# Reordering the mixing stage and the layer boundary of a two-block transformer

## The chip, the core and the metric

One core of a Trainium2 chip runs the whole program. The metric is the device time of one execution in microseconds. The kernel before was timed three times: 1442.81, 1445.81 and 1448.04, median 1445.81.

## What is computed

Two blocks of two layers each work on the same x of 256 rows (SEQ) by 1024 (D_MODEL), in float32. The change lies in the first block and at the start of the second. Of a layer of the first block, this matters:

```python
h = rms_norm(x, norm_mix[l])
proj = h @ w_in[l]                     # q, k, v of two attentions, and gate_logits
y_a = dilated_attention(dq, dk, dv) @ w_proj_a[l]               # 256 wide output, then 1024
y_b = stick_breaking_attention(sq, sk, sv) @ w_proj_b[l]
gates = jax.nn.sigmoid(gate_logits + b_gate[l])
mixed = gates[..., :D_MODEL] * y_a + gates[..., D_MODEL:] * y_b
x = x + mixed @ w_out[l]
h = rms_norm(x, norm_ffn[l])
x = x + conv_ffn(h, w_up[l], conv_w[l], conv_b[l], w_down[l])
```

After the two layers x is normalized, and the second block begins. It also normalizes a memory (256 rows) and multiplies it with weights into keys and values for a later cross attention.

## The kernel before

**Numbers in two parts.** Every float32 operand of a large product is split into a high part (rounded to fp32r) and a low part, the rest. A product is three matmuls: high by high, high by low weight, low by high weight. Activations are 256 rows, two tiles (tt) of 128; their parts are in ahi and alo, or in mhi and mlo, eight blocks of 128 columns each.

**Weights.** They come in chunks of 1 MB through three buffers (raw), in the order of a plan made ahead; SP asks for chunk n once both halves of chunk n-3 are split. Each chunk has two halves of 1024 columns per partition. ACT makes a half's high part (split_half, L1603) and DVE the low one (L2044), each into one of four slots (HL); ACT waits until PE is done with the half four before. Both engines call split_half(m) at written places in their programs, which splits every half up to m that is not split yet. Counted from f0, the first half of the gates' weights, halves 16 and 17 belong to projection b, 18 and 19 to projection a, 20 to 23 to the first column half of w_out ("out1", 0) and 24 to 27 to its second.

**Turning.** PE needs activations turned. A stream turns four groups of four 128 by 128 blocks (turn_blocks, L1005, into PSUM bank 4 or 5), ACT copies a group's high part out (stream_hi), DVE its low part (stream_lo), and PE waits for the low part of the group that the next half chunk needs. turn_to(i) turns all groups up to i; half_chunk calls need before and turn_to after its products, two groups ahead.

**Order.** The program of each engine is written out by hand, and an instruction stands behind all those written before it. Semaphores tie the engines together. Around the change, in one layer of the first block:

1. PE runs the dilated attention. Between its units it does gate products and the product with w_proj_b (between_heads, two half chunks of 12 matmuls). DVE then normalizes the attention output into o_nat (L2161).
2. PE turns branch a (four blocks), ACT takes the high part (L1635), DVE the low (L2081). PE waits for it, then runs w_proj_a as column_chunk (L970 to L972): columns 0 to 511 and then 512 to 1023, in each the two weight halves outside and the two row tiles inside, so that both tiles of a column end together.
3. ACT applies one sigmoid to the gates of branch b (L1759), takes the turned branch a, splits two weight halves, and applies the other sigmoid (L1762). DVE multiplies gates and products: branch b in place (L2299), branch a into o_nat (L2306), and adds the two (L2310, which raises "mixed").
4. PE turns the mixed blocks (stream "mix", into mhi and mlo) and runs out1: groups 0 and 1 ahead of the first half chunk, groups 2 and 3 behind the first and second. DVE's order is: split 20, mix column 0, split 21, low parts of groups 0 and 1, mix column 1, splits 22 and 23, low parts of groups 2 and 3.
5. DVE adds the product to x (L2330). PE turns x for the feed-forward part (stream "xf"), runs it, and ends with the last "down" chunk, also a column_chunk. DVE adds it to x (L2420), PE turns x for the next layer (stream "x1"), and DVE's low parts (L2071) let the next layer's first product (L897) begin.

At the start of the second block, ACT scales the memory's values (memory_product, L1700) in layer 0 ahead of the high parts of the stream "x2" (L1628, L1629).

## Time and profile before

| what | value |
|---|---|
| median of 3 runs | 1445.81 us |
| profiled execution, own time | 1443.27 us |
| its span, first to last instruction | 1441.4 us |
| PE, PEld busy | 1398.6 us, 1190.4 us |
| DVE, ACT, POOL busy | 1016.5 us, 737.9 us, 91.0 us |
| mean granted TensorE clock | 0.998 |
| read from HBM | 239.09 MB |

The profile shows one execution. PE's busy time counts pipelined matmuls whose ends are modelled: one of 512 columns lasts 0.39 us in the records while the next starts 0.23 after it. So the starts are what counts, and the idle time in brackets behind a row is the gap after the modelled end. An arrow in those brackets names the engine and the line that ended the gap.

### The profile page before, as it was taken

The numbers are of one execution on the slowest core, as the hardware profiler recorded it, in microseconds if no ns is written. First come the engines' busy times: TensorE is split into PE (matmuls) and PEld (weight loads), VectorE is DVE, ScalarE is ACT, GpSimd is POOL, SyncE is SP. The second block draws the span as 40 slices with busy tenths as digits, with TensorE's granted clock in tenths as the row PEclk, the third lists the DMA queues.
The fourth block names the chain that finished last, engine by engine and source line by source line (L and its number), as shares of the span: only waits on it lengthen the run. The fifth ranks groups of instructions, "written<-read, shape, count | busy, mean of one in ns | idle before, by whom it ended". The sixth has DMA issues, their size and how long they took to land.

```text
span 1441.4 us, 20319 instructions
## 1 busy us (share of the span) xinstructions
PE 1398.6 (97%) x7936; PEld 1190.4 (83%) x7936; DVE 1016.5 (71%) x1525; ACT 737.9 (51%) x1126; POOL 91.0 (6%) x94
## 2 busy tenths in 40 slices
PE   8999999999999999999999999899999999899997
PEld 6899888888788988888887777788888877788886
DVE  5566678777755657877787676786676657786665
ACT  4563555555455454554555565554445455554443
POOL 0000001000000000211012011100000000100000
PEclk9999999999999999999999999999999999999999
DMA  9734446565454425756647304368865505265552
GB/s 298 248 121 147 135 159 203 179 203 201 153 199 153 140 88 176 240 190 198 204 176 212 111 30 146 104 204 221 220 188 188 175 1 173 91 205 176 194 193 81
DMA packets 154434, 242.36 MB, mean 168 GB/s; under 512 B 4506, under 2 KB 107050, under 8 KB 154076
## 3 DMA queue, kind: packets, MB, share of 16 engines
q1 hardware_dynamic: 150624, 227.23, 48.2%
q0 software_dynamic: 3712, 13.84, 3.7%
q8 instruction: 63, 1.03, 0.3%
q14 instruction: 31, 0.25, 0.1%
q10 hardware_dynamic: 4, 0.01, 0.0%
HBM read 239.09 MB, written 1.97 MB: 167 GB/s over the span
## 4 chain that ended last, share of the span: by engine, by line
PE 90%; DVE 5%; ACT 2%; POOL 1%; issue 1%; DMA 0%; SPq 0%; DVEq 0%; ACTq 0%; POOLq 0%
PE ps L931 19%; PE ps L897 16%; PE ps L904 16%; PE ps L901 16%; PE ps L934 9%; PE ps L1005 3%; PE ps L1083 2%; PE ps L1059 2%; PE ps L1074 1%; DVE wlo L2044 1%; PE ps L970 1%; PE ps L972 1%; PE ps L971 1%; POOL rstd L759 1%; ACT whi L1603 1%
## 5 line engine op out<-in xcount | busy, mean ns | idle before, releaser
L2044 DVE TENSOR_TENSOR wlo<-raw,whi 128x1024 fp32r<-128x1024 f32 (+1 forms) x432 | 539.2, 1259 | 208.1 <-ACT whi L1603 207.6
L1603 ACT CAST whi<-raw 128x1024 fp32r<-128x1024 f32 (+1 forms) x432 | 446.0, 1042 | 269.8 <-PE ps L904 167.8
L931 PE MATMUL ps<-act,whi 128*128 128x512 f32 x1184 | 324.9, 395 | 1.7 <-DVE wlo L2044 1.3
L897 PE MATMUL ps<-whi,mhi 128*128 128x512 f32 (+2 forms) x688 | 236.4, 392 | 4.0 <-DVE mlo L2068 2.2
L931 PEld LDWEIGHTS ps<-act,whi 128*128 128x128 f32 x1184 | 204.8, 189 | 32.4 <-DVE wlo L2044 2.0
L904 PE MATMUL ps<-whi,mlo 128*128 128x512 f32 (+2 forms) x688 | 231.3, 385 | 0.0
L901 PE MATMUL ps<-wlo,mhi 128*128 128x512 f32 (+2 forms) x688 | 231.1, 385 | 0.0
L934 PEld LDWEIGHTS ps<-act,wlo 128*128 128x128 f32 x1184 | 182.5, 189 | 25.7
L934 PE MATMUL ps<-act,wlo 128*128 128x256 f32 x1184 | 189.4, 281 | 0.0
L897 PE MATMUL ps<-whi,act 128*128 128x256 f32 (+1 forms) x512 | 169.1, 330 | 1.5 <-DVE act L2071 1.5
L901 PE MATMUL ps<-wlo,act 128*128 128x256 f32 (+1 forms) x512 | 165.5, 323 | 0.0
L904 PE MATMUL ps<-whi,act 128*128 128x256 f32 (+1 forms) x512 | 165.4, 323 | 0.0
L904 PEld LDWEIGHTS ps<-whi,mlo 128*128 128x128 f32 x688 | 129.2, 188 | 26.7
L901 PEld LDWEIGHTS ps<-wlo,mhi 128*128 128x128 f32 x688 | 129.4, 188 | 26.0 <-issue 0.2
L897 PEld LDWEIGHTS ps<-whi,mhi 128*128 128x128 f32 x688 | 125.5, 188 | 29.1 <-DVE mlo L2068 3.9
L897 PEld LDWEIGHTS ps<-whi,act 128*128 128x128 f32 x512 | 97.5, 190 | 12.1 <-DVE act L2071 2.5
L904 PEld LDWEIGHTS ps<-whi,act 128*128 128x128 f32 x512 | 97.3, 190 | 7.7
L901 PEld LDWEIGHTS ps<-wlo,act 128*128 128x128 f32 x512 | 97.5, 190 | 7.2
L1652 ACT ACTIVATE work<-work,low 128x128 f32<-128x128 f32 (+3 forms) x80 | 41.0, 513 | 65.7 <-DVE low L2110 65.3
L759 POOL TENSOR_TENSOR rstd<-ss,small 128x2 f32<-128x2 f32 (+1 forms) x22 | 25.8, 1171 | 755.1 <-DVE ss L2094 373.9
L802 POOL TENSOR_TENSOR work<-work 128x512 f32<-128x512 f32 x22 | 33.4, 1516 | 272.8 <-DVE work L2350 265.1
L1083 PE MATMUL ps<-proj,work 128*128 128x64 f32 (+1 forms) x336 | 44.5, 273 | 3.2 <-ACT work L1680 2.5
(263 smaller groups left out, 1477.5 us busy)
## 6 DMA issues: line engine op xcount, KB each, us to landing
raw<-in_mlp_w SPq DMA_DIRECT2D x64, 1024.0 KB, 5.4
raw<-in_w_up SPq DMA_DIRECT2D x44, 1024.0 KB, 5.2
raw<-in_w_in SPq DMA_DIRECT2D x39, 1024.0 KB, 5.1
raw<-in_w_down SPq DMA_DIRECT2D x22, 1024.0 KB, 4.9
raw<-in_ev_w_in SPq DMA_DIRECT2D x10, 1024.0 KB, 5.1
raw<-in_w_out SPq DMA_DIRECT2D x8, 1024.0 KB, 4.9
raw<-in_xa_wkv SPq DMA_DIRECT2D x4, 1024.0 KB, 5.3
raw<-in_ev_w_out SPq DMA_DIRECT2D x4, 1024.0 KB, 5.0
```

Source lines behind the costliest of these rows:

```text
L759: nc.gpsimd.tensor_tensor(dst, src, small[:, 0, 0:src.shape[-1]], ALU.pow).then_inc(rstd_ready, 1)
L802: nc.gpsimd.tensor_tensor(two(up_as), two(up_a), row, ALU.mult).then_inc(a_scaled, 1)
L897: nc.tensor.matmul(o, hi[:, kx, rows_], wh[:, k, c0:c0 + w], start=first and h == 0 and k == 0 and (tt == 0 or at[1] == 0), stop=False)
L901: nc.tensor.matmul(o, hi[:, kx, rows_], wl[:, k, c0:c0 + w], start=False, stop=False)
L904: mm = nc.tensor.matmul(o, lo[:, kx, rows_], wh[:, k, c0:c0 + w], start=False, stop=final and h == 1 and k == kh - 1 and (tt == 1 or at[1] ...
L931: nc.tensor.matmul(both, wh[:, k, w], act2[:, kx].rearrange("p i n -> p (i n)"), start=kx == 0, stop=False)
L934: mm = nc.tensor.matmul(top, wl[:, k, w], act2[:, kx, 0], start=False, stop=kx == KD - 1)
L1005: mm = nc.tensor.transpose(bank[:, j * P:j * P + P], src, ident)
L1083: mm = nc.tensor.matmul(o, values_of(u, d)[:, b * P:b * P + P], v, start=b == 0, stop=b == len(d["pv"]) - 1)
L1603: nc.scalar.copy(whi[:, m % HL, 0:w], raw[:, n % RAW, h * w:h * w + w]).then_inc(hi_done, 1)
L1652: nc.scalar.activation(step_of(1536, u, d), step_of(0, u, d), ACT.Exp, scale=-1.0, bias=low[:, d["qt"], s:s + 1], accum_out=den[:, d["qt"] ...
L2044: nc.vector.tensor_tensor(wlo[:, m % HL, 0:w], raw[:, n % RAW, h * w:h * w + w], whi[:, m % HL, 0:w].bitcast(F32), ALU.subtract).then_inc( ...
```

## The change

- ACT applies both sigmoids, branch b's and then branch a's, before it takes the turned branch a, with one split between.
- PE turns branch a inside projection b's second half chunk, between the two tiles.
- column_chunk does its blocks tile by tile: (column 0, tile 0), (0, 1), (1, 0), (1, 1), both weight halves in each, and raises a semaphore for each block. It can run something between (1, 0) and (1, 1). All users of it change order: w_proj_a, the last down of both layers and the last w2 of both layers of the second block.
- The stream "mix" goes to ahi and alo. Its groups 0 and 1 are turned inside w_proj_a's chunk, group 2 inside half chunk 1 of out1 and group 3 inside half chunk 2.
- DVE adds each tile of the mix right after its product. Its order becomes: mix column 0, split 20, low parts of groups 0 and 1, the rest of branch b, mix column 1, split 21, low part of group 2, split 22, low part of group 3, split 23.
- The turning of x's first half for layer 1 stands inside the last down chunk of layer 0; ACT's and DVE's parts for it move to the end of layer 0.
- ACT scales the memory's values behind the first two high groups of "x2" in layer 0 too.

```diff
+MIX_BANKS = (4, 5), (6, 7)
...
-            if c == 0 and key in by_columns:
-                eng.wait_ge(cols_out, TT * by_columns.index(key) + tt + 1)
+            if key in by_columns:
+                if tt == c == 1:
+                    eng.wait_ge(pe_out, 4 * plan.jobs[key][-1] + 4)
+                else:
+                    eng.wait_ge(cols_out, 3 * by_columns.index(key) + 2 * c + tt + 1)
...
-                    stream["turn_to"](place + 2)
+                    stream["turn_to"](place + stream["ahead"])
...
                 for c in range(2):
-                    for h in range(2):
-                        m = 2 * n + h
-                        if c == 0:
-
-                            pe.wait_ge(lo_done, m + 1)
-                        wh, wl = (w[:, m % HL, 512 * c:512 * c + 512] for w in (whi, wlo))
-                        for tt in range(TT):
+                    for tt in range(TT):
+                        o = ps[:, bank(tt, c), :]
+                        for h in range(2):
+                            m = 2 * n + h
+                            if c == tt == 0:
+
+                                pe.wait_ge(lo_done, m + 1)
+                            wh, wl = (w[:, m % HL, 512 * c:512 * c + 512] for w in (whi, wlo))
...
+                            if c == tt == 1:
+                                m0.then_inc(pe_out, 1)
+                                m1.then_inc(pe_out, 1)
                             elif h == 1:
-                                mm.then_inc(cols_out, 1)
+                                m1.then_inc(cols_out, 1)
+                        if inside and c == 1 and tt == 0:
+                            inside()
...
+                def attended():
+
+                    pe.wait_ge(o_ready, o_counts["dil", l])
+                    turn_branch("a")
...
+                                   middle=attended if h else None)
...
                 attention(("dil", l), between_heads)
-                pe.wait_ge(o_ready, o_counts["dil", l])
-                turn_branch("a")
                 pe.wait_ge(grp_dve, plan.by_number[plan.groups["y1", l, "a"]][2])
...
-                tall_job(("pa", l), mhi, mlo, 0, lambda tt, c: 4 + 2 * c + tt, True, True)
-                sx = stream("mix", l, o_nat, lambda h: pe.wait_ge(mixed, 4 * l + 2 * h + 2))
+                sm = stream("mix", l, o_nat, lambda h: pe.wait_ge(mixed, 4 * l + 2 * h + 2), ahead=1)
+                tall_job(("pa", l), mhi, mlo, 0, lambda tt, c: MIX_BANKS[c][tt], True, True, inside=lambda: sm["turn_to"](1))
...
-                wide_job(("out1", l, 0), mhi, mlo, [yb(0, 0), yb(1, 0)], stream=sx)
-
-                wide_job(("out1", l, 1), mhi, mlo, [yb(0, 1), yb(1, 1)], before={2: lambda: sf["turn_to"](1)})
+                wide_job(("out1", l, 0), ahi, alo, [yb(0, 0), yb(1, 0)], stream=sm, middles={1: lambda: sm["turn_to"](2), 2: lambda: sm["turn_to"](3)})
+
+                wide_job(("out1", l, 1), ahi, alo, [yb(0, 1), yb(1, 1)], before={2: lambda: sf["turn_to"](1)})
...
-                    tall_job(("down", l, b), mhi, mlo, 2 * (b % 4), lambda tt, c: yb(tt, c), b == 0, b == NFB - 1)
+                    tall_job(("down", l, b), mhi, mlo, 2 * (b % 4), lambda tt, c: yb(tt, c), b == 0, b == NFB - 1,
+                             inside=(lambda: sx["turn_to"](1)) if l + 1 < DEPTH else None)
...
-                nc.scalar.activation(gates[:, :, D:2 * D], gates[:, :, D:2 * D], ACT.Sigmoid).then_inc(gate_done, 1)
+                for c0 in (D, 0):
+                    nc.scalar.activation(gates[:, :, c0:c0 + D], gates[:, :, c0:c0 + D], ACT.Sigmoid).then_inc(gate_done, 1)
+                split_half(f0 + 2 * NGC + 4)
                 take(("y1", l, "a"), blocks(mhi, 0))
                 split_half(f0 + 2 * NGC + 5)
-                nc.scalar.activation(gates[:, :, 0:D], gates[:, :, 0:D], ACT.Sigmoid).then_inc(gate_done, 1)
-                stream_hi("mix", l, mhi, gs=(0, 1))
+                stream_hi("mix", l, ahi, gs=(0, 1))
                 split_half(f0 + 2 * NGC + 7)
-                stream_hi("mix", l, mhi, gs=(2, 3))
+                stream_hi("mix", l, ahi, gs=(2, 3))
...
+                else:
+                    split_half(n0 + 3)
+                    stream_hi("x1", l + 1, ahi, row=gain_row["x1", l + 1], gs=(0, 1))
...
-                if l == 0:
-                    memory_product(l, "v", 6)
                 stream_hi("x2", l, mhi, row=gain_row["x2", l], gs=(0, 1))
-                if l:
-                    memory_product(l, "v", 6)
+                memory_product(l, "v", 6)
...
                 dve.wait_ge(gate_done, 2 * l + 1)
-                n = gate_b(0)
+                gate_b(0, 0)
                 lo_of(("y1", l, "a"), mhi, mlo, 0)
-                n1 = gate_b(1)
+                gate_b(0, 1)
+                gate_b(1, 0)
+                dve.wait_ge(gate_done, 2 * l + 2)
+                gate_a(0)
                 split_half(f0 + 2 * NGC + 4)
-                dve.wait_ge(gate_done, 2 * l + 2)
-                gate_a(0, n)
+                stream_lo("mix", l, ahi, alo, gs=(0, 1))
+                gate_b(1, 1)
+                gate_a(1)
                 split_half(f0 + 2 * NGC + 5)
-                stream_lo("mix", l, mhi, mlo, gs=(0, 1))
-                gate_a(1, n1)
+                stream_lo("mix", l, ahi, alo, gs=(2,))
+                split_half(f0 + 2 * NGC + 6)
+                stream_lo("mix", l, ahi, alo, gs=(3,))
                 split_half(f0 + 2 * NGC + 7)
-                stream_lo("mix", l, mhi, mlo, gs=(2, 3))
...
                 for c in range(2):
                     for tt in range(TT):
+                        if c == tt == 1 and l + 1 < DEPTH:
+                            stream_lo("x1", l + 1, ahi, alo, row=gain_row["x1", l + 1], gs=(0, 1))
                         product(("down", l, NFB - 1), tt, c)
```

2 * NGC is 16, so f0 + 2 * NGC + 4 is half 20. gate_b(c, tt) now does one tile; gate_a(c) waits for a tile's product, multiplies, waits for that, adds and raises "mixed", and then does the other tile.

## Rows read from the trace of the kernel before

**Rows 1.** The page: share of PE, and the weight loads of w_out (KB, us to landing)
```profile
PE 1398.6 (97%) x7936; PEld 1190.4 (83%) x7936; DVE 1016.5 (71%) x1525; ACT 737.9 (51%) x1126; POOL 91.0 (6%) x94
...
raw<-in_w_out SPq DMA_DIRECT2D x8, 1024.0 KB, 4.9
```

**Rows 2.** The waits of PE: us in total, times, longest us
```profile
PE ps L970 <- DVE mlo L2081: 2.8, 2, 1.4
```

**Rows 3.** Timeline, PE, layer 0's mixing stage (start, us, engine, line, operation, tiles, count)
```profile
161.88 0.60 PE L1005 MATMUL ps<-cst,o_nat 128*128 128x128 f32 x4
...
163.89 0.50 PE L970 MATMUL ps<-whi,mhi 128*128 128x512 f32 x1 [1.41 <-DVE mlo L2081]
...
169.51 1.09 PE L1005 MATMUL ps<-cst,o_nat 128*128 128x128 f32 x8
...
171.57 0.50 PE L897 MATMUL ps<-whi,mhi 128*128 128x512 f32 x1 [0.96 <-DVE mlo L2068]
...
174.69 0.66 PE L1005 MATMUL ps<-cst,o_nat 128*128 128x128 f32 x4
...
175.10 0.47 PE L897 MATMUL ps<-whi,mhi 128*128 128x512 f32 x1
...
183.88 0.39 PE L897 MATMUL ps<-whi,mhi 128*128 128x512 f32 x1
```

**Rows 4.** The timeline, DVE, the same stage
```profile
160.01 0.43 DVE L2161 TENSOR_TENSOR o_nat<-ps,rden 128x256 f32<-128x256 f32 x1
...
162.08 0.69 DVE L2299 TENSOR_TENSOR region<-ps,region 128x512 f32<-128x512 f32 x1 [0.62 <-PE ps L904]
...
166.84 1.29 DVE L2306 TENSOR_TENSOR o_nat<-ps,region 128x512 f32<-128x512 f32 x2 [0.68 <-ACT region L1762]
...
168.17 1.29 DVE L2310 TENSOR_TENSOR o_nat<-o_nat,region 128x512 f32<-128x512 f32 x2
...
169.38 1.22 DVE L2044 TENSOR_TENSOR wlo<-raw,whi 128x1024 fp32r<-128x1024 f32 x1
...
170.82 1.29 DVE L2068 TENSOR_TENSOR mlo<-ps,mhi 128x512 fp32r<-128x512 f32 x2 [0.23 <-ACT mhi L1626]
```

**Rows 5.** The timeline, ACT, the same stage
```profile
151.23 1.05 ACT L1603 CAST whi<-raw 128x1024 fp32r<-128x1024 f32 x1 [0.99 <-PE ps L904]
...
155.99 1.92 ACT L1759 ACTIVATE region<-region 128x2048 f32<-128x2048 f32 x1
...
162.51 0.60 ACT L1635 ACTIVATE mhi<-ps 128x512 fp32r<-128x512 f32 x1 [4.61 <-PE ps L1005]
...
170.21 1.07 ACT L1626 CAST mhi<-ps 128x512 fp32r<-128x512 f32 x2 [3.40 <-PE ps L1005]
```

**Rows 6.** The timeline, DVE and PE, end of layer 0
```profile
377.96 1.40 DVE L2420 SCALAR_TENSOR_TENSOR x<-ps,rstd,x 128x512 f32<-128x512 f32 x2
...
380.98 1.04 PE L1005 MATMUL ps<-cst,x 128*128 128x128 f32 x8
...
383.49 0.50 PE L897 MATMUL ps<-whi,act 128*128 128x512 f32 x1 [1.47 <-DVE act L2071]
```

**Rows 7.** The timeline, PE, ACT and DVE, where the second block begins
```profile
757.83 1.06 PE L1005 MATMUL ps<-cst,x 128*128 128x128 f32 x8
...
758.09 0.84 ACT L1700 ACTIVATE region<-ps,rstd 128x256 f32<-128x256 f32 x2 [1.99 <-PE ps L904]
...
758.82 0.47 ACT L1628 ACTIVATE mhi<-ps,gains 128x256 fp32r<-128x256 f32 x1
...
759.76 1.66 DVE L2071 SCALAR_TENSOR_TENSOR mlo<-ps,gains,mhi 128x256 fp32r<-128x256 f32 x4 [0.70 <-ACT mhi L1629]
```

**Rows 8.** Busy by stretch: length, PE, PEld, DVE, ACT, POOL, clock, DMA share, GB/s
```profile
758.60:763.60 5.00, 3.20 (x16) 2.40 (x15) 4.30 (x7) 3.68 (x7) 2.75 (x5) 1.00 0.75 149
...
1182.00:1185.20 3.20, 2.02 (x17) 1.89 (x17) 1.26 (x5) 1.88 (x6) 0.00 (x0) 1.00 0.01 3
1185.80:1189.20 3.40, 3.40 (x15) 2.79 (x15) 0.61 (x2) 0.59 (x1) 0.00 (x0) 0.52 0.00 0
```

More of the change, by code:

```diff
@@ L948, in spread_row, with wide_job @@
                 mm.then_inc(row_out, 1)
-            def wide_job(key, hi, lo, banks, n=512, stream=None, before={}, ks=(0, KD // 2)):
+            def wide_job(key, hi, lo, banks, n=512, stream=None, before={}, ks=(0, KD // 2), middles={}):
                 ids = plan.jobs[key]
@@ L955, in wide_job, with column_chunk @@
                             before[2 * j + h]()
-                        half_chunk(i, h, hi, lo, ks[j], [[(0, n, banks[tt])] for tt in range(TT)], j == 0, j == len(ids) - 1, stream)
-            def column_chunk(n, hi, lo, k0, bank, first):
+                        half_chunk(i, h, hi, lo, ks[j], [[(0, n, banks[tt])] for tt in range(TT)], j == 0, j == len(ids) - 1, stream,
+                                   middle=middles.get(2 * j + h))
+            def column_chunk(n, hi, lo, k0, bank, first, inside=None):
@@ L975, in column_chunk @@
+                            m1 = nc.tensor.matmul(o, xl, wh, start=False, stop=h == 1)
+                            if c == tt == 1:
+                                m0.then_inc(pe_out, 1)
+                                m1.then_inc(pe_out, 1)
                             elif h == 1:
-                                mm.then_inc(cols_out, 1)
-            def tall_job(key, hi, lo, k0, bank, first, final, between=None, stream=None):
+                                m1.then_inc(cols_out, 1)
+                        if inside and c == 1 and tt == 0:
+                            inside()
@@ L979, in tall_job @@
+            def tall_job(key, hi, lo, k0, bank, first, final, between=None, stream=None, inside=None):
                 ids = plan.jobs[key]
@@ L981, in tall_job @@
                     if key in by_columns and i == ids[-1]:
-                        column_chunk(i, hi, lo, k0 + 2 * j, bank, first and j == 0)
+                        column_chunk(i, hi, lo, k0 + 2 * j, bank, first and j == 0, inside)
                         continue
@@ L1011, in spare, with stream @@
                     nc.tensor.matmul(ps[:, bank, :], ident_b[:], ident_b[:].unsqueeze(1).to_broadcast([P, 4, P]), start=True, stop=True)
-            def stream(tag, l, src, ready, gs=(0, 1, 2, 3), spares=(0, 0, 0)):
+            def stream(tag, l, src, ready, gs=(0, 1, 2, 3), spares=(0, 0, 0), ahead=2):
                 turned, waited = [0], [0]
@@ L1030, in need @@
                     while waited[0] <= i:
-                        turn_to(waited[0] + 1)
+                        turn_to(waited[0] + ahead - 1)
                         if waited[0] == 0 and spares[1]:
@@ L1036, in need @@
                         waited[0] += 1
-                return dict(turn_to=turn_to, need=need, place=gs.index)
+                return dict(turn_to=turn_to, need=need, place=gs.index, ahead=ahead)
             def x_half(n):
@@ L1147, in turn_conv @@
                                  start=True, stop=True).then_inc(pe_grp, 1)
+            sx = stream("x1", 0, x, lambda h: pe.wait_ge((x_in, x_rest_in)[h], 16), spares=(0, 6, 0))
             for l in range(DEPTH):
[L1151 removed]
                 def turn_qk(g):
@@ L1279, in _ @@
                     sm["turn_to"](3)
+                else:
+                    sx = stream("x1", l + 1, x, x_half(x_count("ffn", l)))
                 down(NFB - 1)
@@ L2294, in _, with gate_b, gate_a @@
                     norm_out(("dil", l), HG * qt, HG, heads_of(o_nat, qt, 0, HG), TT * HG)
-                def gate_b(c):
-                    for tt in range(TT):
-                        product(("pb", l), tt)
-                        gt = gates[:, tt, D + 512 * c:D + 512 * c + 512]
-                        n = mark(nc.vector.tensor_tensor(gt, ps[:, yb(tt, c), :], gt, ALU.mult))
-                    return n
-                def gate_a(c, n):
+                def gate_b(c, tt):
+                    product(("pb", l), tt)
+                    gt = gates[:, tt, D + 512 * c:D + 512 * c + 512]
+                    return mark(nc.vector.tensor_tensor(gt, ps[:, yb(tt, c), :], gt, ALU.mult))
+                def gate_a(c):
                     for tt in range(TT):
```

21 lines of the change are left out of this document (8 added, 13 removed).

## Prediction

> **What bounds the kernel now.** I read the page first: PE is busy for 97% of the span [rows 1], and PE's pieces make nearly all of the chain that ended last. The added or removed products are nil, so the change can only win or lose PE's gaps. The waits of PE come next: the first product of projection a (L970) waits 1.4 us for the low part of the turned attention output, once in each layer [rows 2]. Then the timeline of layer 0 around it, engine by engine [rows 3 to 5]. PE turns the four blocks of branch a at 161.88, starts projection a at 163.89, turns the first mixed blocks at 169.51, starts the output product at 171.57 and its second column half at 183.88. Layer 1 shows the same pair of waits, so what is worked out here counts twice.
>
> Two prices recur. The 24 products of 512 columns from 163.89 to 169.51 take 5.62 us, so six take 1.40 and a half chunk of twelve 2.80. A turning of four blocks occupies PE for 0.41 (174.69 to 175.10), one of eight about 0.8 [rows 3].
>
> On DVE [rows 4] a 512 wide operation starts 0.60 after the one before it; where it waits for that one's end, 0.73 (the two L2306 start at 166.84, L2310 at 168.17: 1.33). A split of a weight half takes 1.22. A consumer starts 0.05 after its signal (L2310 ends 169.46, PE turns at 169.51). A product reaches DVE 0.20 after PE has moved on (161.88 to 162.08). From a turning's start to the high part on ACT is 0.63 to 0.70 [rows 3, 5], from there to the low part on DVE 0.61.
>
> **The mixing stage, part by part, layer 0.** *Turning of branch a inside projection b.* The output is normalized at 160.44, so PE turns at 160.49. With 0.41 and the six products left over PE is free at 162.30. *Both sigmoids at once.* The first ends at 157.91, the second, at 1.92 more, at 159.83; the split that now follows takes 1.05 [rows 5] and ends by 160.88, ahead of the turned blocks at 161.12. So it costs nothing; without that cover it would cost up to its own 1.92. The high part ends 161.72, the low part 162.44, and projection a starts at 162.50 instead of 163.89: 1.39 won.
>
> *Column blocks tile by tile.* Block (column 0, tile 0) ends 163.90, tile 1 at 165.30. DVE multiplies at 164.10, adds at 164.83, multiplies at 165.50, adds at 166.23, ends 166.92. PE has finished (column 1, tile 0) at 166.70, waits 0.27, turns eight blocks to 167.77, and ends projection a at 169.17. *Output product, half 0.* The high parts start at 167.67, the low parts at 168.28, behind the split of half 20 (counted from the gates' first half), which ends 168.05. Half 0 runs 169.17 to 171.97, against a start at 171.57 before.
>
> *What is late next.* DVE's new order puts the rest of branch b's product (0.60), both tiles of the second column (2 x 1.33) and only then the split of half 21 behind the low parts. From 169.49: 170.10, 172.76, 173.98. PE needs it at 171.97 and starts half 1 at 174.04: **2.07 lost**. Before, that split stood ahead of the low parts, at 169.38 [rows 4], and PE never asked for it.
>
> Then the turnings inside halves 1 and 2 close a loop. Group 2 is turned at 175.44 after six products; PE goes on to 177.25. Its low part starts 1.31 after the turning, at 176.75, and DVE's program has the split of half 22 behind it: 177.36 to 178.58. PE starts half 2 at 178.64: **1.39 lost**. Half 3 repeats it: turned 180.04, low part 181.35, split 23 to 183.18, PE free 181.85, start 183.24: **1.39 lost**. Half 3 ends at 186.04. Before it was 183.88 [rows 3]. **The stage costs 2.16 more per layer, 4.32 in both.**
>
> I see nothing later that gives this back: the next splits, the additions to x and the turning of the next stream hang on these halves and move with them. The weights for halves 26 and 27 are asked for once half 21 is split, 3.4 us later than before. With 4.9 us to land [rows 1] they are there by 179.1, and ACT, which converts half 26 behind group 3's high part, comes to it at about 183; that is hidden. SP's later loads have the same cover, and POOL's one added delay, the memory rows it loads behind mix group 3, has most of the feed-forward part to hide it.
>
> **The layer boundary** [rows 6]. Today (DVE's first pair of L2420) x's first half is ready at 379.36, PE turns it only at 380.98 behind the last product, and the next layer's first product starts at 383.49, 2.51 after that turning. Moved ahead of the last six products, the turning starts at 379.58 (380.98 less 1.40). The chain then gives 382.09; PE itself is free at 381.78. So **1.40 is won**. The last addition to x now waits behind two low groups on DVE (1.66, as [rows 7] show for such a pair) and ends near 383.5. PE asks for it at 384.9, after half 0, so it is covered. If that cover went, it would cost at most its own 1.66.
>
> **Memory's scaling** [rows 7]. The x2 turning starts at 757.83; ACT is in the scaling until 758.82, when the high parts begin. They could start 0.64 to 0.70 after the turning, at 758.47 to 758.53; DVE sat idle 0.70 ahead of the low part, so it follows. **0.35 won**, bounds 0.29 and 0.70. The scaling itself then stands in front of the next splits, whose products are over 5 us away.
>
> **Column order elsewhere.** The last chunk of both downs and both last w2 chunks change order too. Only a tile's middle blocks come 0.7 earlier; the last block ends when it did, and x waits for that one: 0. The half buffers come free up to 0.7 later, and the second half's split is asked for 0.7 earlier; in all these chunks it was done before the chunk began. Bounds: 0.3 either way for all four. Later signals for each tile instead of for each pair cost DVE about 0.1 per column, which is in the sum above.
>
> **The sum** against the profiled execution of 1443.27 (span 1441.4): +4.32 - 1.40 - 0.35 = +2.57, so 1445.8. The median of the runs, 1445.81, lies 2.5 above that execution, so on the scale of the median the forecast is **1448.4**, 0.2% slower. About 0.3%, 4.3 us, is what a measurement of this kernel can tell from no change.
>
> **Rivals.**
> *The splits are not late (clean version).* If halves 21 to 23 were split when PE asks, half 0's start at 169.17 plus four halves and two turnings, 12.02, ends the product at 181.19, 2.69 earlier than before. Twice that with the other two gains is -7.1: **1438.7**. For it: ACT can have made half 21's high part by 163.5, long before it is wanted, so only DVE's order stands in the way. Against it: its instructions run in the order written, and the split of 21 stands behind 2.66 us of mixing that itself needs the last block but two of projection a. Chance 0.15.
>
> *The clock falls (ends slower).* Place: halves 1 to 3, where PE would rest 2.07, 1.39 and 1.39 us in some 14. Where the granted clock fell in this trace, PE had been busy 2.02 of 3.20 us with small products; it then ran 3.4 us at 0.52, which is the 1.2 GHz level, a loss of about 1.6 [rows 8]. Once in each layer is +3.3: **1451.7**; twice in each, 1455. It decides if the share of work there, 9.2 of 14 us, is too low. Against it: a stretch with only 3.20 busy of 5.00 [rows 8] kept the full clock. Chance 0.13. The Trainium skill's TensorE: Matmul & The Clock Gate (section "Why this matters for your kernels") warns that idle gaps between bursts of matmuls send the clock back to half rate; it speaks against this change, and the trace has one case on each side. By that rule, if it applied here, the time would be the one just given.
>
> *The opening gain does not arrive.* If the turning inside projection b catches the attention output late, or the second sigmoid is still in ACT's way, projection a starts at 163.89 as before and everything behind it moves by 1.39 per layer: **1451.2**. For it: only 0.24 us lie between ACT's split and the turned blocks. Against it: being 0.24 late costs only the excess. Chance 0.08.
>
> **How the numbers follow.** Forecast 0.64, clean 0.15, clock 0.13, opening 0.08. Within the forecast, each of the three stalls may be off by 0.3 per layer, 1.8 in all, and the two medians by about 1.5, so its own range is 1446 to 1451. The range of all, 1442.5 to 1453, leaves out the clean version and the worst of the clock. Faster by over 0.3% (under 1441.5): the clean version, nearly whole, 0.13. Slower (over 1450.1): the two slow rivals and a tenth of the forecast, 0.22. Between them 0.65.
>
> **What would show it.** Right: PE's wait at L970 gone; waits of the output product's halves 1, 2, 3 for the weight's low part (DVE L2044), near 2.1, 1.4 and 1.4 us, twice; the output product some 2.2 longer to its end; the wait at the boundary shrunk from 1.47 to a few tenths. Wrong: no wait on L2044 there (clean), a granted clock under 1.00 in the stage (clock), or the turning of branch a later than 0.1 behind DVE's L2161 (opening). The prediction fails outright if the stage shortens or if a stall of over 1 us stands anywhere outside it.

## The result and the profile after

| | before | changed |
|---|---|---|
| median, 20 runs each, one chip | 1443.89 us (1441.74 to 1448.19) | 1447.96 us (1446.04 to 1452.66) |
| ratio, 95% interval | | 1.0029 [1.0018, 1.0040] |
| profiled execution, its span | 1443.27, 1441.4 | 1446.46, 1444.6 |
| DVE, ACT busy | 1016.5, 737.9 | 1016.7, 738.0 |
| mean granted clock | 0.998 | 0.997 |

The change costs 4.1 us, 0.29%. The work is the same (7936 matmuls, busy times within 0.5 us), so what is lost lies in gaps of PE and in its clock. The waits of PE in the profile of the changed kernel (us in total, times, longest) name them at once:

```profile
PE ps L901 <- DVE wlo L2060: 8.8, 6, 1.9
...
PE ps L901 <- DVE mlo L2087: 1.5, 1, 1.5
...
PE ps L1013 <- DVE o_nat L2322: 0.4, 2, 0.2
```

The 1.4 us for the turned attention output, twice in [rows 2], is gone. In its place the output product waits for the low part of its weights, six times, 8.8 us. The timeline of PE in layer 0 of the changed kernel shows where:

```profile
161.74 0.64 PE L1013 MATMUL ps<-cst,o_nat 128*128 128x128 f32 x4
...
163.80 0.50 PE L975 MATMUL ps<-whi,mhi 128*128 128x512 f32 x1
...
168.36 1.09 PE L1013 MATMUL ps<-cst,o_nat 128*128 128x128 f32 x8 [0.17 <-DVE o_nat L2322]
...
175.49 0.47 PE L901 MATMUL ps<-whi,act 128*128 128x512 f32 x1 [1.91 <-DVE wlo L2060]
176.96 0.60 PE L1013 MATMUL ps<-cst,o_nat 128*128 128x128 f32 x4
180.18 0.47 PE L901 MATMUL ps<-whi,act 128*128 128x512 f32 x1 [1.24 <-DVE wlo L2060]
181.64 0.60 PE L1013 MATMUL ps<-cst,o_nat 128*128 128x128 f32 x4
184.87 0.47 PE L901 MATMUL ps<-whi,act 128*128 128x512 f32 x1 [1.23 <-DVE wlo L2060]
...
187.71 0.39 PE L901 MATMUL ps<-whi,act 128*128 128x512 f32 x1
```

The stage begins 1.23 later here (the attention output is ready at 161.67, not 160.44), because the program's first 155 us took 1.2 longer in this execution (most of it a fall of the clock near 28 us, see below). The reader is to subtract that: 26.04 from the attention output to the last row, against 23.44 before [rows 3, 4]. DVE's timeline shows why PE waits:

```profile
168.22 1.22 DVE L2060 TENSOR_TENSOR wlo<-raw,whi 128x1024 fp32r<-128x1024 f32 x1
169.67 1.29 DVE L2084 TENSOR_TENSOR act<-ps,act 128x512 fp32r<-128x512 f32 x2 [0.23 <-ACT act L1640]
170.88 0.68 DVE L2315 TENSOR_TENSOR region<-ps,region 128x512 f32<-128x512 f32 x1
171.48 0.68 DVE L2321 TENSOR_TENSOR o_nat<-ps,region 128x512 f32<-128x512 f32 x1
...
173.52 0.69 DVE L2322 TENSOR_TENSOR o_nat<-o_nat,region 128x512 f32<-128x512 f32 x1
174.13 1.22 DVE L2060 TENSOR_TENSOR wlo<-raw,whi 128x1024 fp32r<-128x1024 f32 x1
178.21 0.69 DVE L2084 TENSOR_TENSOR act<-ps,act 128x512 fp32r<-128x512 f32 x1 [2.87 <-ACT act L1640]
178.82 1.22 DVE L2060 TENSOR_TENSOR wlo<-raw,whi 128x1024 fp32r<-128x1024 f32 x1
182.90 0.69 DVE L2084 TENSOR_TENSOR act<-ps,act 128x512 fp32r<-128x512 f32 x1 [2.87 <-ACT act L1640]
```

The split of half 21 (174.13) stands behind the mix of column 1. The next two are worse than late: DVE sits idle for 2.87 us in front of a low part that waits for a turning, with a split it could have done standing right behind it. An engine with idle time is no proof that it cannot hold another up.

The two edges gained. The first rows are PE at the end of layer 0, the others PE at the start of the second block:

```profile
383.43 1.04 PE L1013 MATMUL ps<-cst,x 128*128 128x128 f32 x8
...
385.87 0.50 PE L901 MATMUL ps<-whi,act 128*128 128x512 f32 x1
...
762.89 1.06 PE L1013 MATMUL ps<-cst,x 128*128 128x128 f32 x8
...
765.43 0.51 PE L901 MATMUL ps<-whi,mhi 128*128 128x512 f32 x1 [1.47 <-DVE mlo L2087]
```

The wait of 1.47 at the boundary [rows 6] is gone. From the end of the block (column 1, tile 0) to the next layer's first product is 2.44, where it was 2.51 and the six products of 1.37 more. The wait of 1.80 at the second block is 1.47. The prediction had a stall of over 1 us outside the stage as a sign against itself. Taken by its words the sign is there, but this wait is an old one that got shorter. The others of over 1 us (3.0 at the start, 1.3, 1.1 and 1.1) stood in the kernel before within 0.2 us of that, so no new one has come.

**A ruler for all runs.** ACT loads its tables at fixed places of the program: the sigmoid's ahead of the mixing stage, the Silu's behind it. In the changed kernel, layer 0:

```profile
155.92 1.28 ACT L1775 ACT_TABLE_LOAD   x1
...
216.62 1.28 ACT L1817 ACT_TABLE_LOAD   x1
```

The distance holds the mixing stage and nothing else of the change. The table gives it for every kernel profiled, with the distance from Silu (layer 0) to sigmoid (layer 1), which holds the boundary, and from Silu (layer 1) to the second block's first table load, which holds memory's scaling. The last column tells where the granted clock was under 1.00 in stretches of 4 us near these places.

| kernel | mixing 0 | mixing 1 | boundary | second block's start | clock fell near |
|---|---|---|---|---|---|
| before | 58.1 | 58.1 | 311.2 | 249.3 | |
| before, second profile (e12) | 58.1 | 58.1 | 311.2 | 250.9 | 762 |
| changed | 60.7 | 60.7 | 309.9 | 249.0 | |
| changed again (e9) | 61.9 | 61.7 | 309.9 | 249.0 | 175, 546 |
| e1, splits earlier | 56.8 | 56.8 | 309.9 | 249.0 | |
| e2, split 21 earlier | 59.2 | 59.2 | 309.9 | 249.0 | |
| e3, mixing alone | 61.5 | 62.0 | 311.2 | 250.9 | 175, 547, 769 |
| e4, edges alone | 58.1 | 58.1 | 309.9 | 249.0 | |
| e5, e3 filled | 60.7 | 60.7 | 311.3 | 249.3 | |
| e6, e1 with sigmoids apart | 58.0 | 58.0 | 309.9 | 249.0 | |
| e7, e1 with branch a turned behind | 58.1 | 58.1 | 309.9 | 249.0 | |
| e8, e1 with branch b first | 56.2 | 56.2 | 309.9 | 249.0 | |
| e10, changed filled | 60.7 | 60.7 | 309.9 | 249.0 | |
| e11, column order alone | 58.1 | 58.1 | 311.3 | 249.3 | |

At full clock these lengths repeat within 0.1 us, where medians of the whole kernel scatter by over 5. So small terms are read from here: the change costs 2 x 2.6 in the mixing stage and wins 1.3 and 0.3 at the edges, 3.5 net (from unrounded starts). The two spans differ by 3.2, and what else differs goes with falls of the clock. The changed kernel's profile has one near 28 us (a clock of 0.67 from 28 to 32; e8, e10 and e11 have it too) that the other lacks, and its start took 1.2 longer. The profile of the kernel before has one near 1186 us (0.71 from 1184 to 1188) that the other lacks, and its part behind 831 us, of which the change touches only the column order, took 1.6 longer.

That last part, from the second block's first table load to the end, shows where much of the scatter of all these kernels comes from. Every profile has a low clock in the last 12 us. Apart from that the clock falls there at none, one, two or all of three places, near 935, 1190 and 1250. The part took 608.3 to 608.5 us in the five profiles with no such fall (changed, e4, e5, e9, e11), 609.8 to 610.5 in the four with one (before, e1, e2, e8), 611.3 to 611.4 in the three with two (e3, e7, e10), and 612.7 and 613.0 in the two with three (e6, e12).

### The profile page after: what moved, and what is told of

Read it like the earlier page. It is cut to its first block, busy times and chain, and to the rows that moved or that the text cites. A ratio compares the mean times of both kernels' runs of the same rounds, so it can differ in the third digit from the quotient of the medians.

```text
span 1444.6 us, 20319 instructions
## 1 busy us (share of the span) xinstructions
PE 1399.1 (97%) x7936; PEld 1188.8 (82%) x7936; DVE 1016.7 (70%) x1525; ACT 738.0 (51%) x1126; POOL 91.1 (6%) x94
## 4 chain that ended last, share of the span: by engine, by line
PE 89%; DVE 6%; ACT 2%; POOL 1%; issue 1%; DMA 0%; SPq 0%; DVEq 0%; ACTq 0%; POOLq 0%
PE ps L935 19%; PE ps L901 16%; PE ps L908 16%; PE ps L905 16%; PE ps L938 9%; PE ps L1013 3%; PE ps L1091 2%; PE ps L1067 2%; DVE wlo L2060 1%; PE ps L1082 1%; POOL rstd L763 1%; PE ps L975 1%; PE ps L977 1%; PE ps L976 1%; ACT whi L1617 1%
## 5 line engine op out<-in xcount | busy, mean ns | idle before, releaser
L901 PE MATMUL ps<-whi,mhi 128*128 128x512 f32 (+2 forms) x624 | 210.8, 392 | 2.1 <-DVE mlo L2087 1.5
L908 PE MATMUL ps<-whi,mlo 128*128 128x512 f32 (+2 forms) x624 | 206.4, 385 | 0.0
L905 PE MATMUL ps<-wlo,mhi 128*128 128x512 f32 (+2 forms) x624 | 206.2, 385 | 0.0
L901 PE MATMUL ps<-whi,act 128*128 128x256 f32 (+1 forms) x576 | 195.6, 340 | 8.8 <-DVE wlo L2060 8.8
L908 PE MATMUL ps<-whi,act 128*128 128x256 f32 (+1 forms) x576 | 191.0, 332 | 0.0
L905 PE MATMUL ps<-wlo,act 128*128 128x256 f32 (+1 forms) x576 | 190.7, 331 | 0.0
L908 PEld LDWEIGHTS ps<-whi,mlo 128*128 128x128 f32 x624 | 117.2, 188 | 24.1
L905 PEld LDWEIGHTS ps<-wlo,mhi 128*128 128x128 f32 x624 | 117.3, 188 | 23.8 <-issue 0.2
L901 PEld LDWEIGHTS ps<-whi,mhi 128*128 128x128 f32 x624 | 113.3, 188 | 24.4 <-DVE mlo L2084 2.0
L901 PEld LDWEIGHTS ps<-whi,act 128*128 128x128 f32 x576 | 109.7, 190 | 24.3 <-issue 12.2
L908 PEld LDWEIGHTS ps<-whi,act 128*128 128x128 f32 x576 | 109.5, 190 | 10.5
L905 PEld LDWEIGHTS ps<-wlo,act 128*128 128x128 f32 x576 | 109.8, 191 | 9.6
```

The source lines that it names most:

```text
L901: nc.tensor.matmul(o, hi[:, kx, rows_], wh[:, k, c0:c0 + w], start=first and h == 0 and k == 0 and (tt == 0 or at[1] == 0), stop=False)
L905: nc.tensor.matmul(o, hi[:, kx, rows_], wl[:, k, c0:c0 + w], start=False, stop=False)
L908: mm = nc.tensor.matmul(o, lo[:, kx, rows_], wh[:, k, c0:c0 + w], start=False, stop=final and h == 1 and k == kh - 1 and (tt == 1 or at[1] ...
```

## The experiments

e1 to e4 ran on one chip, e5 to e8 on a second, e9 to e11 on a third and e12 on the second again, each group with fresh runs of the kernel before beside it.

**e1: the splits one place earlier.**

```diff
                 stream_lo("mix", l, ahi, alo, gs=(0, 1))
+                split_half(f0 + 2 * NGC + 5)
                 gate_b(1, 1)
                 gate_a(1)
-                split_half(f0 + 2 * NGC + 5)
-                stream_lo("mix", l, ahi, alo, gs=(2,))
                 split_half(f0 + 2 * NGC + 6)
-                stream_lo("mix", l, ahi, alo, gs=(3,))
+                stream_lo("mix", l, ahi, alo, gs=(2,))
                 split_half(f0 + 2 * NGC + 7)
+                stream_lo("mix", l, ahi, alo, gs=(3,))
```

> Changed kernel with DVE's splits of weight halves 21, 22 and 23 each one place earlier: 21 behind the first low parts, 22 behind the mix of column 1, 23 behind the low part of group 2. Theory (the splits stand too late): the three waits on DVE L2060 in each layer (1.9, 1.24 and 1.23 us) go; some 0.5, 0.2 and 0.3 remain, since the mix of column 1 is now 1.1 later and a low part still follows its turning. The output product's first column half ends about 3.8 earlier in each layer, 7.6 in all: about 3.5 below the kernel before, ratio near 0.9976. Rival (DVE simply has too much to do in the stage; moving a split moves the mix, and PE waits for that instead): within 1.5 us of the changed kernel, ratio near 1.002 to 1.003.

1438.24 (1437.29 to 1439.43) against 1444.92, ratio 0.9953 [0.9938, 0.9969]. The stage is 3.9 shorter than the changed kernel's in each layer; 3.8 was expected. Of PE's waits in the stage only those for the mix are left; here PE in layer 0:

```profile
167.16 1.09 PE L1013 MATMUL ps<-cst,o_nat 128*128 128x128 f32 x8 [0.19 <-DVE o_nat L2322]
...
174.20 0.66 PE L1013 MATMUL ps<-cst,o_nat 128*128 128x128 f32 x4 [0.46 <-DVE o_nat L2322]
177.75 0.60 PE L1013 MATMUL ps<-cst,o_nat 128*128 128x128 f32 x4
```

Three moved lines turn 0.3% slower into 0.5% faster. The theory stands, and the rival (DVE has too much to do) is out. By the ruler e1 is 4.3 below the kernel before (2 x 1.3 and the edges' 1.7). The medians differ by 6.7, where 3.5 was expected. The five runs spread over 2.1 us and those of the kernel before over 5.6, so fewer falls of the clock may be the rest; that was not shown.

**e2: only the split of half 21 earlier**, halves 22 and 23 left.

```diff
                 stream_lo("mix", l, ahi, alo, gs=(0, 1))
+                split_half(f0 + 2 * NGC + 5)
                 gate_b(1, 1)
                 gate_a(1)
-                split_half(f0 + 2 * NGC + 5)
                 stream_lo("mix", l, ahi, alo, gs=(2,))
```

> Changed kernel with only the split of half 21 moved, to behind the first low parts. Theory: the 1.9 us wait goes, a wait of about 0.5 for the mix of column 1 comes at the turning of group 2, and the other two waits on L2060, 1.24 and 1.23, stand as they are, for they come from the low part that waits for a turning: 1.5 less per layer than the changed kernel, 3.0 in all, about 1 above the kernel before. Rival (the three waits are one debt of DVE, handed on from half to half): with the first gone the later ones shrink too, or the first wait reappears at half 2; the total falls by more than 4, or by less than 1.

1444.52 (1441.7 to 1446.51) against 1444.92, ratio 0.9995 [0.9984, 1.0005]. The stage is 59.2, 1.5 less than the changed kernel's, as expected. The two later waits did not move by more than 0.01; PE in layer 0:

```profile
174.49 0.66 PE L1013 MATMUL ps<-cst,o_nat 128*128 128x128 f32 x4 [0.47 <-DVE o_nat L2322]
...
177.77 0.47 PE L901 MATMUL ps<-whi,act 128*128 128x512 f32 x1 [1.23 <-DVE wlo L2060]
179.23 0.60 PE L1013 MATMUL ps<-cst,o_nat 128*128 128x128 f32 x4
182.46 0.47 PE L901 MATMUL ps<-whi,act 128*128 128x512 f32 x1 [1.23 <-DVE wlo L2060]
```

The rival's number, a total lower by more than 4, is not excluded by the medians: by the two ratios, from different chips, the total fell by 4.9. The rows decide against it, since with the first wait gone the later ones neither shrank nor grew. So the three waits are not one debt handed on. The first is a queue behind the mix. Each of the others is a closed loop: PE's turning, ACT's high part, DVE's low part, and the split behind it, against six products of PE.

**e3: the mixing stage alone**, and **e4: the edges alone.** e3 is the changed kernel with the parts of the diff for the stream "x1" and for memory_product undone, e4 the one with those for the sigmoids, branch a's turning, the stream "mix" and DVE's mixing order undone.

```diff
-            sx = stream("x1", 0, x, lambda h: pe.wait_ge((x_in, x_rest_in)[h], 16), spares=(0, 6, 0))
             for l in range(DEPTH):
+                sx = stream("x1", l, x, x_half(x_count("ffn", l - 1)) if l else lambda h: pe.wait_ge((x_in, x_rest_in)[h], 16), spares=(0, 0 if l else 6, 0))
...
-                    if l == 0 or g >= 2:
-                        stream_lo("x1", l, ahi, alo, row=gain_row["x1", l], gs=(g,))
+                    stream_lo("x1", l, ahi, alo, row=gain_row["x1", l], gs=(g,))
```

> Changed kernel with the layer boundary and memory's scaling as before: the mixing stage and the column order alone. By the sum on record: 4.3 above the kernel before, ratio 1.003. If the two edges brought their 1.75 and the measured 4.1 is right, the stage must have cost more than the sum says: 5.8, ratio 1.004. Rival (the edges brought nothing): 4.1, as the changed kernel.

1449.12 (1447.47 to 1453.33) against 1444.92, ratio 1.0036 [1.0023, 1.0048], 5.2 more. The interval holds all three of the numbers expected, 4.1, 4.3 and 5.8, so the lengths must decide. Its profile had the clock fall in both mixing stages and at 769. With the 2.6 of the changed kernel's first profile the stage costs 5.2 in both layers; the 4.3 of the sum was short by 0.9.

```diff
-                sm = stream("mix", l, o_nat, lambda h: pe.wait_ge(mixed, 4 * l + 2 * h + 2), ahead=1)
-                tall_job(("pa", l), mhi, mlo, 0, lambda tt, c: MIX_BANKS[c][tt], True, True, inside=lambda: sm["turn_to"](1))
+                tall_job(("pa", l), mhi, mlo, 0, lambda tt, c: MIX_BANKS[c][tt], True, True)
+                sm = stream("mix", l, o_nat, lambda h: pe.wait_ge(mixed, 4 * l + 2 * h + 2))
```

> Kernel before with the column order, the turning of x inside the last down chunk and memory's scaling behind the high parts; the mixing stage in its old order. By the sum on record: 1.75 below the kernel before, ratio 0.9988, with 1.4 at the boundary (the wait of 1.47 at the first product of layer 1 down to about 0.3) and 0.35 at the second block's start. Rival (what is won there is lost later in layer 1): ratio 1.000.

1440.70 (1439.86 to 1444.96) against 1444.92, ratio 0.9976 [0.9965, 0.9986], 3.5 less, twice what was expected. By the ruler the edges bring 1.3 and 0.3, and nothing is lost in layer 1. The other 1.9 is not in the lengths at full clock.

**e5: the mixing stage alone, its rests filled.** The first run with a low clock in the stage was e3's. Its busy time and granted clock by stretch, layer 0 (length, then PE, PEld, DVE, ACT, POOL busy, the clock, DMA share, GB/s):

```profile
171.80:174.00 2.20, 0.34 (x2) 0.00 (x0) 2.09 (x3) 0.00 (x0) 0.00 (x0) 1.00 0.01 4
174.00:178.00 4.00, 3.93 (x13) 3.24 (x14) 0.38 (x1) 0.59 (x1) 0.00 (x0) 0.63 0.61 234
```

PE rests at 1.00 and runs the products that follow at 0.63, most of them at the 1.2 GHz level. The idle matmuls go between:

```diff
-                wide_job(("out1", l, 0), ahi, alo, [yb(0, 0), yb(1, 0)], stream=sm, middles={1: lambda: sm["turn_to"](2), 2: lambda: sm["turn_to"](3)})
+                wide_job(("out1", l, 0), ahi, alo, [yb(0, 0), yb(1, 0)], stream=sm, middles={1: lambda: sm["turn_to"](2), 2: lambda: sm["turn_to"](3)},
+                         before={1: lambda: spare(6, 1), 2: lambda: spare(4, 1), 3: lambda: spare(4, 1)})
```

> The mixing stage alone (as in the run of that name) with idle matmuls of 512 columns into a free bank ahead of the output product's half chunks 1, 2 and 3 (6, 4 and 4 of them, 1.4, 0.9 and 0.9 us by 0.23 each), inside waits of 1.9, 1.2 and 1.2 us. They compute nothing that is used. Theory (the clock falls behind the stalls in some executions, as in the profile of the mixing stage alone, at 174 and 546 us): no granted clock under 1.00 in the stage, which then takes 60.7 from table load to table load in both layers instead of 61.5 and 62.0, and a median 1 to 2 below that run. Rival (the clock's fall there is chance and has nothing to do with the rests): median within 0.5 of it, and falls as often.

1449.29 (1446.79 to 1450.61) against 1443.56, ratio 1.0038 [1.0025, 1.0050]. The profile is as the theory has it: 60.7 in both layers, no low clock but in the last 12 us. The median is the rival's: no gain over e3's ratio of 1.0036. One good profile and five runs that do not agree leave it open, so it was tried again on the changed kernel (e10).

**e6: the sigmoids apart; e7: branch a turned behind projection b; e8: branch b's last tile first.** All three start from e1.

```diff
-                for c0 in (D, 0):
-                    nc.scalar.activation(gates[:, :, c0:c0 + D], gates[:, :, c0:c0 + D], ACT.Sigmoid).then_inc(gate_done, 1)
-                split_half(f0 + 2 * NGC + 4)
+                nc.scalar.activation(gates[:, :, D:2 * D], gates[:, :, D:2 * D], ACT.Sigmoid).then_inc(gate_done, 1)
                 take(("y1", l, "a"), blocks(mhi, 0))
                 split_half(f0 + 2 * NGC + 5)
+                nc.scalar.activation(gates[:, :, 0:D], gates[:, :, 0:D], ACT.Sigmoid).then_inc(gate_done, 1)
```

> The kernel with the splits one place earlier, but the two sigmoids apart again, branch a's behind the turned branch a and two splits. Theory (both at once is what keeps ACT out of the way): branch a's sigmoid ends about 0.9 later than DVE wants it for the mix of column 0, the first mixed blocks are turned 0.9 later, 1.8 in both layers. Rival (it is covered by PE's own products): 0 to 0.4 in all.

1441.35 (1439.83 to 1444.3) against 1443.56, ratio 0.9984 [0.9974, 0.9994]. The stage is 58.0 instead of 56.8: 1.2 per layer, 2.4 in all, 0.6 more than expected. The wait for the mix at the first turning is the one that grew (waits of PE, whole execution; the two of 0.5 at group 2 are among the four):

```profile
PE ps L1013 <- DVE o_nat L2321: 3.7, 4, 1.4
```

```diff
                 attention(("dil", l), between_heads)
+                pe.wait_ge(o_ready, o_counts["dil", l])
+                turn_branch("a")
                 pe.wait_ge(grp_dve, plan.by_number[plan.groups["y1", l, "a"]][2])
...
-                                   middle=attended if h else None)
```

> The kernel with the splits one place earlier, but branch a turned behind projection b as before, not inside it. Theory (the sum on record: 1.39 per layer): PE waits about 1.4 again for L2097 ahead of projection a, 2.8 slower in both layers. Rival (the stage is bound by DVE's chain, which starts at the attention output and not at PE): under 1 in all.

1441.17 (1439.21 to 1443.52) against 1443.56, ratio 0.9974 [0.9964, 0.9983]. The stage is 58.1: 1.3 more per layer than e1. The old wait is back at its old length:

```profile
PE ps L975 <- DVE mlo L2093: 2.8, 2, 1.4
```

```diff
                 gate_b(1, 0)
+                gate_b(1, 1)
                 dve.wait_ge(gate_done, 2 * l + 2)
...
                 split_half(f0 + 2 * NGC + 5)
-                gate_b(1, 1)
                 gate_a(1)
```

> The kernel with the splits one place earlier, and the last tile of branch b's product on DVE moved ahead of the mix of column 0, into an idle time of 0.46 there. Theory: the mix of column 0 comes 0.15 later, that of column 1 0.45 earlier, the wait of 0.46 at the turning of group 2 goes: 0.3 won per layer, 0.6 in all. Rival (the wait at the first turning, 0.19, grows by all that is won): 0.

1438.09 (1437.34 to 1438.69) against 1443.56, ratio 0.9961 [0.9949, 0.9974]. The stage is 56.2, 0.6 less than e1's per layer where 0.3 was expected, and the shortest of all. e1 and e8 ran on different chips, so their medians are not compared; by the ruler e8 is 1.1 ahead, 5.4 below the kernel before. Both beat the kernel before and the changed one.

**e9: the changed kernel again, e10: it filled, e11: the column order alone**, on one chip. e10's edit is e5's. e11 is the kernel before with column_chunk, its signals and wait_product as changed.

> The changed kernel once more, beside the two that follow on one chip. In its 20 timed runs the mean granted clock was 0.996 to 0.998 where the time was 1446.0 to 1448.1, and 0.991 to 0.995 where it was 1447.8 to 1452.7. Theory (falls of the clock make the scatter): the profile's time follows its granted clock by about 1 us for 0.001, from 1444 to 1445 at 1.000. Rival (the scatter is of another kind, DMA say): a profile with a low clock and a low time, or the reverse.

1447.27 (1445.37 to 1451.7) against 1443.54, ratio 1.0027 [1.0015, 1.0039]. This profile, of 1446.83, had the clock fall in both stages, at the same place as e3's, and nowhere else but in the last 12 us. Layer 0, the same columns as for e3, and layer 1:

```profile
171.80:174.00 2.20, 0.38 (x2) 0.36 (x3) 1.68 (x2) 0.00 (x0) 0.00 (x0) 1.00 0.00 0
174.00:178.00 4.00, 4.00 (x14) 3.22 (x13) 0.38 (x1) 0.59 (x1) 0.00 (x0) 0.57 0.76 261
543.00:546.00 3.00, 1.09 (x5) 0.61 (x4) 2.28 (x3) 0.00 (x0) 0.00 (x0) 1.00 0.00 0
546.00:550.00 4.00, 4.00 (x14) 3.22 (x13) 0.73 (x2) 0.59 (x1) 0.00 (x0) 0.57 0.79 262
```

The stage took 61.9 and 61.7 instead of 60.7, so a fall costs 1.0 to 1.3 here (0.8 and 1.3 in e3). It costs less than the 1.7 that a clock of 0.57 over 4 us takes, since slower products eat into the rest behind them (PE, layer 0):

```profile
173.62 0.47 PE L901 MATMUL ps<-whi,act 128*128 128x512 f32 x1 [1.92 <-DVE wlo L2060]
...
175.91 1.05 PE L1013 MATMUL ps<-cst,o_nat 128*128 128x128 f32 x4
...
179.58 0.47 PE L901 MATMUL ps<-whi,act 128*128 128x512 f32 x1 [0.92 <-DVE wlo L2060]
```

The turning of four blocks lasts 1.05 instead of 0.60, and the wait that was 1.24 is 0.92. Over the eleven runs the slope of the rule holds: those at 0.998 took 1445.4 and 1445.9, those at 0.992 1450.8 to 1451.7. Its starting point was about 1 too high: at 0.996 it gives 1448 to 1449, and the profile took 1446.83. No low clock came with a low time, so the rival is out.

> The changed kernel with idle matmuls (6, 4, 4) in the rests ahead of half chunks 1 to 3 of the output product. Theory (the rests there let the clock fall in half of the executions): median 1 to 3 below the changed kernel on the same chip, nearer to its lowest run; none of its time with a clock under 1.00 in the stage. Rival (the falls that make the scatter lie elsewhere, in the second block): medians within 1.

1446.42 (1444.29 to 1450.42) against 1443.54, ratio 1.0015 [1.0005, 1.0026]. The stage took 60.7 twice at full clock, although its profile had falls at 24, 1190 and 1254. Its median is 0.85 under e9's and its lowest run 1.1 under. That is inside the rival's 1 and short of the theory's 1 to 3, and the intervals of the two ratios overlap. The mean clocks of the single runs say more. Of the 31 runs of the changed kernel 13 had one of 0.994 or less (4 of e9's 11, on this chip), of the twelve filled ones none; of e3's ten runs three had, of e5's five none. All four of e9's low ones would fall on its side by chance in one case of 27. So the rests of the stage are very likely what brings the lowest clocks, while the falls in the second block go on without them. What the filling is worth at the median is not settled.

> The kernel before with nothing but the column blocks tile by tile, in all six chunks that use them, nothing run between them. By the sum on record: 0, bounds 0.3 either way; from table load to table load 58.1 in both mixing stages and 248 between. Rival (the later release of half buffers, up to 0.7, holds a split back): up to 0.7 slower behind each of the six, 4 in all, ratio 1.003.

1443.04 (1441.22 to 1447.01) against 1443.54, ratio 0.9997 [0.9987, 1.0006]. 58.1, 58.1, 311.3, 249.3: the column order by itself is worth nothing, as the sum had it. (The 248 expected "between" is neither of the last two distances, which were 311.2 and 249.3 before.) It is the slot for a turning that it opens that counts.

**e12: the kernel before, a second profile**, with no edit.

> The kernel before itself, for a second profile. Its executions scatter from 1441 to 1448, those of the two edges alone mostly lie between 1440 and 1441, though its stages are only 1.75 shorter. Theory (the rest of 1.47 at the layer boundary, of 1.80 at the second block's start or those of 1.41 and 0.96 in the mixing stage let the clock fall in some executions): a granted clock under 1.00 within some 8 us behind one of these places, if this execution is one of the slower ones. Rival (its falls are all in the second block's attention, as in its first profile): nothing at these places, falls near 930, 1185 or 1250 alone.

1444.51 (1441.78 to 1447.72) against 1442.93, ratio 1.0000 [0.9980, 1.0020]: two samples of the same kernel on one chip, six and seven runs, with medians 1.6 apart. The profile is the run of 1447.72. Its clock by stretch at the start of the second block:

```profile
756.00:760.00 4.00, 2.77 (x24) 2.52 (x22) 3.30 (x6) 2.02 (x6) 0.75 (x2) 1.00 0.00 0
760.00:764.00 4.00, 3.42 (x10) 2.70 (x11) 4.00 (x7) 2.16 (x3) 2.00 (x4) 0.72 0.92 188
764.00:766.00 2.00, 2.00 (x10) 1.59 (x9) 0.71 (x1) 0.33 (x1) 0.00 (x0) 0.70 0.62 41
```

The clock fell behind the rest of 1.80, and the stretch took 250.9 instead of 249.3. The same profile also has all three falls of the second block, so the rival's places are there too and cost more, 613.0 instead of 608.4 behind the ruler. e3, with the same old order there, shows the same fall and the same 250.9. Of the five profiles with the old order two fell there; of the nine with memory's scaling behind the high parts, where the rest is 1.47, none did. Two falls dealt out by chance over the 14 would both be among those five in one case of nine, so this is a hint and no proof. The order there may be a part of the 1.9 by which e4's ratio exceeds the ruler's 1.6; the falls near 930, 1190 and 1250 move each median as well. How much is whose was not settled.

## Why the prediction was right

**The mixing stage**, step by step from the output of the attention (160.44 before, 161.67 after). *Branch a inside projection b*: projection a was to start 2.06 later and started 2.13 later; e7 prices the step at 1.3 per layer against 1.39. *Both sigmoids at once*: ACT's split ended 0.5 ahead of the turned blocks, and the step cost nothing. It even earns 1.2 per layer in e6, which the sum had not asked. *The first mixed turning*: to come after 6.53, came after 6.69. *Half 1*: 13.60, came 13.82, with a rest of 1.91 where 2.07 was forecast. *Halves 2 and 3*: 18.20 and 22.80, came 18.51 and 23.20, rests of 1.24 and 1.23 where 1.39 was forecast. (The forecast's rests count from the next start that was free, the profile's from the modelled end of the matmul before; counted as the forecast does they are 2.07, 1.41 and 1.40.) *End*: 25.60, came 26.04.

**What was mis-sized** are small terms of the stage, 0.44 in all: 2.60 per layer against 2.16, the whole stage 5.2 against 4.32. Half of it, 0.22, is there when half 1 starts: DVE's split of half 21 ended 13.68 behind the attention output (13.54 forecast), and PE started 0.14 behind the split's end at 175.35, not 0.06. Halves 2 and 3 add 0.09 each. There too PE starts about 0.14 behind the split, and the six products from the restart to the turning take 1.47 and 1.46 (175.49 to 176.96, 180.18 to 181.64), not 1.40; the chain from the turning to the split's end took back 0.06. The last half adds 0.04. The 0.06 was read from products that waited for a low part; no product of these rows in the kernel before waited for a split.

**The edges**: 1.3 and 0.3 against 1.40 and 0.35. **The column order**: 0, as forecast (e11). The sum at full clock is thus +3.5 against +2.57.

**The rivals.** The clean version failed for the reason given, the place of the splits in DVE's program, and most of it was there to be had: by the ruler e1 is at -4.3 and e8 at -5.4, against -7.1 (by ratio -6.8 and -5.6). The clock rival was right in its mechanism and place, and its chance of 0.13 was too low: two of the three profiles of kernels with the unfilled rest of 1.9 in the stage show the fall in both layers. It was too dear: 1.1 on average (0.8 to 1.3), not 1.6. It is a part of the forecast's execution-to-execution scatter and not an alternative to it. In the 20 runs of the changed kernel the mean clock was 0.996 to 0.998 in ten, of 1446.0 to 1448.1 us, and 0.991 to 0.995 in the other ten, of 1447.8 to 1452.7. The Trainium skill's TensorE: Matmul & The Clock Gate (section "Why this matters for your kernels") warns that idle gaps between bursts of matmuls send the clock back to half rate. Here it fell to 0.63 (e3) and 0.57 (e9) behind rests of 1.9, which are shorter gaps than the section names, and the measurement decides. The opening rival did not occur: branch a was turned 0.07 behind the attention output (161.74 and 161.67).

One sum of the chances does not come out: the two slow rivals and a tenth of the forecast are 0.27, not the 0.22 given for a slower kernel.

The forecast of 1448.4 met 1447.96 more closely than its sum deserves, and that is luck. The median of three runs it was set on, 1445.81, was 1.9 above that of twenty, and the effect itself was 1.5 short (2.6 against 4.1).

## What to carry to other kernels

When a turning is moved into a product, follow what else stands in the helper engine's program behind the instruction that takes the turning's result: ready work that PE will want (here a split of 1.2 us) belongs ahead of an instruction that waits for PE. Read the engine's idle time together with what is next in its program; DVE was idle 2.87 us right in front of the work that PE was waiting for. And measure an edit of a few us by the distance between two fixed events in the profiles, which repeats within 0.1 at full clock, before trusting medians of runs that scatter by 5.

## What the runs showed of the hardware

Behind a rest of PE of 1.8 to 1.9 us in dense work the granted clock fell to the 1.2 GHz level in some executions of a kernel and not in others, at the same place each time (175 and 546 in e3 and e9; 762 and 769 in e12 and e3). In the nine profiles with a rest of 1.47 at 764 it did not fall there. With the rests of the stage filled by unused matmuls it stayed full there in both profiles, and none of 17 runs had a mean clock of 0.994 or less, where 16 of 41 unfilled ones had.

A rest just ahead is not the only thing that goes with a fall. The changed kernel's profile has a clock of 0.50 from 28 to 30 us, with no rest ahead: PE is busy 15.95 of the 16 us from 8 to 24. What stands just ahead is a row of 30 tiny products (8x8 and 16x16 blocks), as in e8 and e10, which have the same fall. The kernel before ran them too and kept the full clock there in both profiles, so what decides stays open.

A fall of the clock costs 0.8 to 1.3 us where waits behind it hide a part, 1.6 at the start of the second block and 1.4 to 2.1 in its later part. How many of these falls an execution has, none to three in that later part, makes 608.3 to 613.0 us out of the same program.
